# Five slots for split weights, a ring of five for raw data, and five half pieces at the end of a stage

## The chip, the cores and the metric

One core of one Trainium2 chip runs the whole program. The metric is device time in microseconds (us) of one execution; lower is better. The kernel before takes 2476.28 us, the median of three runs (2475.11 to 2478.31).

## The reference

Two layers of a decoder block on 256 tokens of width 2048, all in float32. `c_act` is `silu(c)`; `w_in` has 4,956 columns, which are cut into the inputs of three token mixers.

```python
def hybrid_layer(x, ...):
    mod = c_act @ ada_w + ada_b                      # 2048 x 12288 weights, one row of input
    sh_a, sc_a, gt_a, sh_m, sc_m, gt_m = jnp.split(mod[:, None, :], 6, axis=-1)
    h = rms_norm(x, norm_mix) * (1.0 + sc_a) + sh_a
    (cq, ckv, kr, fq, fk, fv, ff, nq, nkc, ...) = jnp.split(h @ w_in, split_points, axis=-1)
    o = concatenate([rms_norm(o_mla), rms_norm(o_fox), rms_norm(o_nsa)])   # three attentions
    x = x + gt_a * (o @ w_out)                       # 2048 x 2048
    h = rms_norm(x, norm_mlp) * (1.0 + sc_m) + sh_m
    u = jnp.square(jax.nn.relu(h @ mlp_w1))          # 2048 x 8192
    return x + gt_m * (u @ mlp_w2)                   # 8192 x 2048
# after two layers: rms_norm(x, final_norm)
```

## The kernel before

All weights are read once. They come in **pieces**: 256 rows by up to 512 columns, up to 512 KB, numbered Q = 0 to 827 in one order (`PIECES`, from `ORDER` and `mlp_order`). A layer has 158 pieces ahead of its MLP (`FRONT`: projections, compression weights `cw1`, output projection `wo0` to `wo3`) and 256 in the MLP.

A piece goes through four engines. SyncE (SP) issues its load into a slot of the raw ring `w_raw` (`load_piece`, L622). ScalarE (ACT) rounds it to the short format, `w_hi` (`hi`, L732). VectorE (DVE) computes the rest, `w_lo = w_raw - w_hi` (`lo`, L1197). TensorE (PE) multiplies in `product`: for both halves m of the 256 tokens and both groups of 128 rows three matmuls, `hi*hi`, `lo*hi`, `hi*lo` (L1668 to L1670), 12 matmuls in a piece; `cw1` pieces take 4 (`compress`, L1688 and L1689).

**Slots.** `w_hi` and `w_lo` have `RING` = 4 slots: `hi` of piece Q waits until PE has finished piece Q-4. `w_raw` has `RAW` = 7 slots, shared by the pieces and by the **ada tiles**, the 512 KB tiles of `ada_w` that DVE multiplies and accumulates itself (`ada_tile`, L1137, first of a block L1134). The load of an entry waits until DVE has consumed the entry `RAW` places earlier in the ring (`slot_free`), by `lo_done` or `ada_used`. `LOADS` sorts the loads by that moment. The first 64 ada tiles have eight slots of their own, and the first 24 pieces are never sorted ahead of `lo` of the piece five earlier.

**Order around a piece.** ACT and DVE run, after `hi(Q)` or `lo(Q)`, the steps listed under `SIDE[Q]`: evacuations, splits of transposed activations, attention steps (`slot`, `exp`), residuals, ada tiles. PE runs the transposes of `PE_POST[Q]` after piece Q. A transpose placed at q has its step on ACT and DVE at q+3 in nearly all cases. Each engine keeps its order, so a step that waits holds back everything behind it.

**Borders.** At the end of a stage (`BORDERS`: pieces 158, 414, 572, 828) the next stage needs the normalised result of the whole previous one. So the last four pieces are done by halves: first tokens 0 to 127 of all four (`product(q, (0,))`), which signals `half_done`, then tokens 128 to 255 of each. While PE does the second halves, `border` has the first half finished: residual (L1300, L1306), squares (ACT, L739), mean (L1166, L1167), power on GpSimd (POOL, L705), scaled copy (`fill`, L1192). PE transposes it (`n1_a` or `n2_a`, L1555) after piece B-2, ACT scales and rounds it (L771, L775), DVE takes the rest (L1311), and then PE starts the next stage: first halves of B, B+1, B+2, transposes of the second half (`_b`), first half of B+3, and then the second halves. The first piece of a stage also waits for its accumulator (`acc_free`): at 158 and 572 it is the one that the residual of the previous stage's last chunk has to leave (L1300 of m = 1); at 414 it is another.

Of the kernel before, what the change touches and what calls it, by code (L numbers as in the profile page):

```python
# [56 lines left out]
SUPERS = 4  # L57
MLP_LEN = SUPERS * 64
LAYER = FRONT + MLP_LEN
RING, RAW = 4, 7  # L60
ALL = LAYERS * LAYER


# [50 lines left out]
def side(Q, step, prio):  # L114
    SIDE.setdefault(Q, []).append((prio, len(SIDE[Q]), step))


def t_step(l, at, name, side_at, bank=0, prio=2, pre=False):

    (PE_PRE if pre else PE_POST).setdefault(at, []).append(("T", l, name))  # L120
    T_BANK[l, name] = bank
    side(side_at, ("T", l, name), prio)
# [17 lines left out]
def border(B, l, chunk, ln, which):  # L140


    side(B - 1, ("resid", l, chunk, 3, 0), 0)
    side(B - 1, ("square", ln, which, 3, 0), 0)
    side(B - 1, ("norm", ln, which, 0), 0)
    if which == "n1" and ln == LAYERS:
        side(B - 1, ("result", 0), 0)
        side(B, ("resid", l, chunk, 3, 1), 0)
        side(B, ("square", ln, which, 3, 1), 0)
        side(B, ("norm", ln, which, 1), 0)  # L150
        side(B, ("result", 1), 0)
        return
    side(B - 1, ("fill", ln, which, 0, 0), 0)
    t_step(ln, B - 2, f"{which}_a", B + 1, 0)
    side(B + 1, ("resid", l, chunk, 3, 1), 3)
    side(B + 2, ("norm", ln, which, 1), 3)
    side(B + 2, ("fill", ln, which, 0, 1), 3)
    side(B + 3, ("square", ln, which, 3, 1), 0)
    t_step(ln, B, f"{which}_b", B + 3, 1, 2, pre=True)
    side(B + 3, ("fill", ln, which, 1), 4)  # L160


for l in range(LAYERS):
# [5 lines left out]
    if l == 0:  # L169
# [4 lines left out]
        for b in range(1, 4):  # L174
            q = 6 * b
# [12 lines left out]
    if l:  # L188
        border(F, l - 1, (SUPERS - 1, 7), l, "n1")
        for b in range(1, 4):  # L190
            t_step(l, F + 6 * b - 5, f"n1_{2 * b}", F + 6 * b - 2, 0)
            t_step(l, F + 6 * b - 4, f"n1_{2 * b + 1}", F + 6 * b - 1, 1)
# [59 lines left out]


    border(M, l, "wo3", l, "n2")
    for b in range(1, 4):
        t_step(l, M + 6 * b - 5, f"n2_{2 * b}", M + 6 * b - 2, 0)
# [33 lines left out]
    for s in range(SUPERS):  # L290
        for j in range(4):
            q = M + 64 * s + 8 * (4 + j) + 10
            if s < SUPERS - 1 or j < 3:
                side(q, ("resid", l, (s, 4 + j), j), 3)
                if s == SUPERS - 1:
                    side(q + (2 if j < 2 else 1), ("square", l + 1, "n1", j), 4)
                    if l == LAYERS - 1:
                        side(q + 3, ("gain", j), 4)
border(ALL, LAYERS - 1, (SUPERS - 1, 7), LAYERS, "n1")

for Q in SIDE:
# [3 lines left out]
BORDERS = [FRONT, LAYER, LAYER + FRONT, ALL]  # L305
# [110 lines left out]
def trunk(nc, x, c, positions, inv_freq, ada_w, ada_b, norm_mix, norm_mlp, w_in, fox_b_f, mla_q_norm, mla_w_uq,  # L416
          mla_kv_norm, mla_w_ukv, nsa_pos_k, nsa_pos_v, cmp_k_w1, cmp_k_w2, cmp_v_w1, cmp_v_w2,
          out_norm, w_out, mlp_w1, mlp_w2, final_norm, out):
    with ExitStack() as ctx:
# [1088 lines left out]
        def _(pe):  # L1508
# [167 lines left out]
            def compress(Q):  # L1676

                l, chunk, p = PIECES[Q]
                j = p // 16
                if p == 0:  # L1680
                    pe.wait_ge(acc_free[1], ACC_USE[l, chunk])
                if p % 16 == 0:
                    pe.wait_ge(split_done, split_value(l, ("kcT", "vcT")[j]))
                pe.wait_ge(lo_done, Q + 1)
                for k in range(2):
                    kt = (p % 16) * 2 + k
                    st = BLK[j][:, 64 * kt:64 * kt + P]
                    pe.matmul(acc[1][:, j, :], st, w_hi[:, Q % RING, k, :], start=kt == 0, stop=False)  # L1688
                    mm = pe.matmul(acc[1][:, j, :], st, w_lo[:, Q % RING, k, :], start=False, stop=kt == 31)  # L1689
                mm.then_inc(piece_used, 1)  # L1690
# [57 lines left out]
            def then(Q):  # L1748

                for kind, l, what in PE_POST.get(Q, []):  # L1750
                    if kind == "csc":
                        compressed_scores(l, what)
                    elif kind == "T" and what != "csc":
                        t_in(l, what)
                    elif kind == "slot":
                        slot(l, what)

            for Q in range(ALL):
                if Q + 4 in BORDERS:
                    for q in range(Q, Q + 4):  # L1760
                        product(q, (0,))
                if Q in BORDERS:
                    for q in range(Q, Q + 3):
                        product(q, (0,))
                    for kind, l, what in PE_PRE[Q]:
                        t_in(l, what)
                    product(Q + 3, (0,))
                elif Q == 0:
                    for kind, l, what in PE_PRE[Q]:
                        t_in(l, what)  # L1770
                if any(B - 4 <= Q < B + 4 for B in BORDERS):
                    product(Q, (1,))
                elif PIECES[Q][1] == "cw1":
                    compress(Q)
                else:
                    product(Q)
                then(Q)
# [25 lines left out]
```

## Time and profile before

| | |
|---|---|
| median of the runs | 2476.28 us |
| the profiled execution | 2472.75 us |
| its span, first to last instruction | 2470.5 us |
| PE, DVE, ACT busy | 96%, 72%, 49% |
| mean granted TensorE clock | 0.989 |
| moved by DMA | 633.91 MB, mean 257 GB/s |

The span is what the profile's views divide; the execution's own time is 2.25 us more. A busy PE is modelled: consecutive 512-column matmuls start 0.23 us apart while each is listed with 0.39 us. In the timeline a bracket at the end of a row tells the idle time of that engine before the instruction and what ended it.

### The profile page before, as it was taken

How to read it: one execution, taken by the hardware profiler on the slowest of the kernel's cores; microseconds unless marked ns; L12 is line 12 of the kernel's file. 1: busy time of each engine (PE TensorE's matmuls, PEld its weight loads, DVE VectorE, ACT ScalarE, POOL GpSimd, SP SyncE). 2: the span in 40 equal slices, each digit the busy share in tenths (PEclk: the TensorE clock that was granted, in tenths of full speed). 3: DMA queues.
4: the chain of work that ended last, by engine and by line, in shares of the span. 5: the costliest groups of instructions: out<-in, count | busy, mean ns of one | idle time of the engine just before them, and what ended most of it. 6: DMA issues, size and time to landing. Idle time of an engine off the chain costs nothing.

```text
span 2470.5 us, 29668 instructions
## 1 busy us (share of the span) xinstructions
PE 2373.6 (96%) x11277; PEld 1969.3 (80%) x11277; DVE 1775.3 (72%) x2116; ACT 1203.5 (49%) x1646; POOL 23.7 (1%) x50
## 2 busy tenths in 40 slices
PE   3799999989999999999999999999999999999998
PEld 3677888768888888888878887878788888888887
DVE  7988988778777777887767788677566455555555
ACT  3256555445534434434445666455553453453453
POOL 1000000000000000000000000000000000000000
PEclk9899999999999999999999999999999999999999
DMA  9979986789889889888867788466577666666663
GB/s 368 382 242 351 314 281 210 256 292 324 286 306 308 291 317 323 304 316 300 296 228 266 264 268 281 137 213 213 180 253 256 188 186 195 185 185 197 187 188 127
DMA packets 318612, 633.91 MB, mean 257 GB/s; under 512 B 20428, under 2 KB 41352, under 8 KB 317832
## 3 DMA queue, kind: packets, MB, share of 16 engines
q1 hardware_dynamic: 314432, 625.49, 75.9%
q10 hardware_dynamic: 4040, 6.54, 0.8%
q8 instruction: 90, 1.47, 0.2%
q14 instruction: 50, 0.41, 0.0%
HBM read 629.85 MB, written 2.10 MB: 256 GB/s over the span
## 4 chain that ended last, share of the span: by engine, by line
PE 84%; DVE 8%; DMA 4%; issue 2%; ACT 2%; POOL 0%; SPq 0%; ACTq 0%; POOLq 0%; DVEq 0%
PE acc L1668 18%; PE acc L1670 18%; PE acc L1669 18%; PE pair L1668 7%; PE pair L1670 7%; PE pair L1669 7%; DMA arena<-in_ada_w 3%; DVE ada_acc L1137 3%; DVE w_lo L1197 2%; PE bank_T L1533 1%; PE bank_T L1578 1%; PE pair L1716 1%; PE bank_O L1533 1%; PE acc L1688 1%; PE acc L1689 1%
## 5 line engine op out<-in xcount | busy, mean ns | idle before, releaser
L1197 DVE TENSOR_TENSOR w_lo<-w_raw,w_hi 128x1024 fp32r<-128x1024 f32 (+3 forms) x828 | 981.5, 1192 | 376.7 <-ACT w_hi L732 376.0
L732 ACT ACTIVATE w_hi<-w_raw 128x1024 fp32r<-128x1024 f32 (+3 forms) x828 | 850.1, 1033 | 729.6 <-PE acc L1670 440.3
L1668 PE MATMUL acc<-w_hi,hT_hi 128*128 128x512 f32 (+3 forms) x1536 | 608.1, 396 | 24.8 <-DVE hT_lo L1311 12.7
L1670 PE MATMUL acc<-w_lo,hT_hi 128*128 128x512 f32 (+3 forms) x1536 | 589.4, 384 | 0.0
L1669 PE MATMUL acc<-w_hi,hT_lo 128*128 128x512 f32 (+3 forms) x1536 | 588.2, 383 | 0.0
L1137 DVE SCALAR_TENSOR_TENSOR ada_acc<-w_raw,silu_c,ada_acc 128x1024 f32<-128x1024 f32 x300 | 383.7, 1279 | 0.7 <-DVE small L1276 0.4
L1668 PEld LDWEIGHTS acc<-w_hi,hT_hi 128*128 128x128 f32 x1536 | 291.3, 190 | 85.3 <-DVE hT_lo L1311 15.6
L1670 PEld LDWEIGHTS acc<-w_lo,hT_hi 128*128 128x128 f32 x1536 | 290.8, 189 | 56.0
L1669 PEld LDWEIGHTS acc<-w_hi,hT_lo 128*128 128x128 f32 x1536 | 291.7, 190 | 51.6 <-issue 1.7
L1668 PE MATMUL acc<-w_hi,uT_hi 128*128 128x512 f32 (+1 forms) x720 | 283.0, 393 | 0.0
L1670 PE MATMUL acc<-w_lo,uT_hi 128*128 128x512 f32 (+1 forms) x720 | 279.6, 388 | 0.0
L1669 PE MATMUL acc<-w_hi,uT_lo 128*128 128x512 f32 (+1 forms) x720 | 279.4, 388 | 0.0
L1668 PE MATMUL pair<-w_hi,hT_hi 128*128 128x512 f32 (+1 forms) x448 | 178.6, 399 | 15.8 <-DVE w_lo L1197 15.8
L1670 PE MATMUL pair<-w_lo,hT_hi 128*128 128x512 f32 (+1 forms) x448 | 173.9, 388 | 0.0
L1669 PE MATMUL pair<-w_hi,hT_lo 128*128 128x512 f32 (+1 forms) x448 | 173.6, 388 | 0.0
L1669 PEld LDWEIGHTS acc<-w_hi,uT_lo 128*128 128x128 f32 x720 | 135.3, 188 | 27.8 <-issue 1.0
L1668 PEld LDWEIGHTS acc<-w_hi,uT_hi 128*128 128x128 f32 x720 | 135.2, 188 | 27.8 <-issue 1.0
L1670 PEld LDWEIGHTS acc<-w_lo,uT_hi 128*128 128x128 f32 x720 | 135.2, 188 | 27.8
L1668 PE MATMUL pair<-w_hi,uT_hi 128*128 128x512 f32 (+1 forms) x352 | 136.6, 388 | 1.5 <-DVE w_lo L1197 1.5
L1670 PE MATMUL pair<-w_lo,uT_hi 128*128 128x512 f32 (+1 forms) x352 | 136.2, 387 | 0.0
L1669 PE MATMUL pair<-w_hi,uT_lo 128*128 128x512 f32 (+1 forms) x352 | 136.1, 387 | 0.0
L1668 PEld LDWEIGHTS pair<-w_hi,hT_hi 128*128 128x128 f32 x448 | 86.0, 192 | 34.6 <-DVE w_lo L1197 19.0
(259 smaller groups left out, 2030.2 us busy)
## 6 DMA issues: line engine op xcount, KB each, us to landing
w_raw<-in_mlp_w SPq DMA_DIRECT2D x512, 512.0 KB, 4.8
w_raw<-in_ada_w SPq DMA_DIRECT2D x320, 512.0 KB, 5.7
w_raw<-in_w_in SPq DMA_DIRECT2D x112, 512.0 KB, 5.0
arena<-in_ada_w SPq DMA_DIRECT2D x64, 512.0 KB, 11.3
w_raw<-in_w_out SPq DMA_DIRECT2D x64, 512.0 KB, 5.6
w_raw<-in_nsa_cmp_k_w SPq DMA_DIRECT2D x32, 512.0 KB, 5.3
w_raw<-in_nsa_cmp_v_w SPq DMA_DIRECT2D x32, 512.0 KB, 5.2
w_raw<-in_w_in SPq DMA_DIRECT2D x16, 388.0 KB, 4.4
```

What stands on the lines that cost most here:

```text
L732: a.activation(w_hi[:, Q % RING, :, 0:n], w_raw[:, i % RAW, :, 0:n], ACT.Copy).then_inc(hi_done, 1)
L1137: ins = v.scalar_tensor_tensor(ada_acc[:], raw, silu_c[:, kt:kt + 1], ada_acc[:], ALU.mult, ALU.add)
L1197: v.tensor_tensor(w_lo[:, Q % RING, :, 0:n], w_raw[:, RING_NO["lo", Q] % RAW, :, 0:n], w_hi[:, Q % RING, :, 0:n].bitcast(F32), ALU.subtrac ...
L1533: mm = pe.transpose(bank[:, k, P * m:P * m + P], halves[m], ident[:])
L1578: mm = pe.matmul(flat_[:, k:k + 1], ada_acc[:, P * k:P * k + P], ones[:, 0:1], start=True, stop=True)
L1668: pe.matmul(o, st_hi[:, kt + k, tok], wh, start=first and k == 0, stop=False)
L1669: pe.matmul(o, st_lo[:, kt + k, tok], wh, start=False, stop=False)
L1670: mm = pe.matmul(o, st_hi[:, kt + k, tok], wl, start=False, stop=last and k == 1)
L1688: pe.matmul(acc[1][:, j, :], st, w_hi[:, Q % RING, k, :], start=kt == 0, stop=False)
L1689: mm = pe.matmul(acc[1][:, j, :], st, w_lo[:, Q % RING, k, :], start=False, stop=kt == 31)
L1716: mm = pe.matmul(o, NQ[:, h, qt], k_[:, h // 4, 0:keys], start=True, stop=True)
```

## The change

`RING` goes from 4 to 5 and `RAW` from 7 to 5: the memory for ten split tiles and five raw ones is that of eight and seven. At a border five pieces instead of four are done by halves, and the transpose of the first half moves from after piece B-2 to after piece B-3.

```diff
-RING, RAW = 4, 7
+RING, RAW = 5, 5
@@ border
-    t_step(ln, B - 2, f"{which}_a", B + 1, 0)
+    t_step(ln, B - 3, f"{which}_a", B + 1, 0)
@@ TensorE
             for Q in range(ALL):
-                if Q + 4 in BORDERS:
-                    for q in range(Q, Q + 4):
+                if Q + 5 in BORDERS:
+                    for q in range(Q, Q + 5):
                         product(q, (0,))
                 if Q in BORDERS:
                     for q in range(Q, Q + 3):
                         product(q, (0,))
...
-                if any(B - 4 <= Q < B + 4 for B in BORDERS):
+                if any(B - 5 <= Q < B + 4 for B in BORDERS):
                     product(Q, (1,))
```

## Rows read from the trace of the kernel before

**Rows 1.** The page: busy share by engine, and GB/s moved in 40 slices

```profile
PE 2373.6 (96%) x11277; PEld 1969.3 (80%) x11277; DVE 1775.3 (72%) x2116; ACT 1203.5 (49%) x1646; POOL 23.7 (1%) x50
...
GB/s 368 382 242 351 314 281 210 256 292 324 286 306 308 291 317 323 304 316 300 296 228 266 264 268 281 137 213 213 180 253 256 188 186 195 185 185 197 187 188 127
```

**Rows 2.** Waits of PE, whole run: total us, times, longest

```profile
PE pair L1668 <- DVE w_lo L1197: 17.3, 11, 3.5
...
PE acc L1668 <- DVE hT_lo L1311: 12.7, 7, 2.0
...
PE acc L1668 <- DVE w_lo L1197: 4.9, 6, 1.6
PE acc L1668 <- DVE ybuf L1300: 4.5, 2, 2.3
```

**Rows 3.** Timeline at the border of piece 414: start, us, engine, line

```profile
1278.64 0.39 PE L1668 MATMUL acc<-w_hi,uT_hi 128*128 128x512 f32 x1
...
1280.00 0.39 PE L1668 MATMUL acc<-w_hi,uT_hi 128*128 128x512 f32 x1
...
1281.65 0.69 DVE L1300 TENSOR_TENSOR ybuf<-acc,arena 128x512 f32<-128x512 f32 x1 [3.16 <-PE acc L1670]
...
1284.86 0.49 DVE L1192 TENSOR_SCALAR ybuf<-X,small 128x512 f32<-128x512 f32 x1 [0.65 <-POOL small L705]
...
1285.49 0.63 PE L1555 MATMUL bank_T<-ident,ybuf 128*128 128x128 f32 x4
...
1287.11 0.40 PE L1670 MATMUL acc<-w_lo,uT_hi 128*128 128x512 f32 x1
...
1289.21 0.47 PE L1668 MATMUL acc<-w_hi,hT_hi 128*128 128x512 f32 x1 [1.71 <-issue]
```

**Rows 4.** Timeline at the border of piece 572

```profile
1739.85 0.40 PE L1670 MATMUL acc<-w_lo,hT_hi 128*128 128x512 f32 x1
...
1741.77 0.68 DVE L1300 TENSOR_TENSOR ybuf<-acc,arena 128x512 f32<-128x512 f32 x1
...
1742.50 0.50 PE L1668 MATMUL acc<-w_hi,hT_hi 128*128 128x512 f32 x1 [2.26 <-DVE ybuf L1300]
```

**Rows 5.** Timeline ahead of the border of piece 158

```profile
534.46 3.48 DVE L1197 TENSOR_TENSOR w_lo<-w_raw,w_hi 128x1024 fp32r<-128x1024 f32 x3
...
535.73 0.50 PE L1668 MATMUL acc<-w_hi,hT_hi 128*128 128x512 f32 x1 [0.24 <-DVE w_lo L1197]
```

**Rows 6.** Windows: busy us by engine, PEclk, DMA share, GB/s

```profile
226.00:256.00 30.00, 29.34 (x174) 24.01 (x173) 27.84 (x38) 18.61 (x33) 0.00 (x0) 1.00 0.99 356
...
478.00:540.00 62.00, 58.27 (x263) 46.15 (x262) 51.48 (x52) 27.61 (x42) 0.69 (x1) 1.00 0.93 319
...
1950.00:2450.00 500.00, 500.00 (x2253) 413.84 (x2252) 266.10 (x229) 233.64 (x252) 0.00 (x0) 1.00 0.60 184
...
1297.00:1301.00 4.00, 4.00 (x12) 3.01 (x11) 1.27 (x2) 0.84 (x1) 0.00 (x0) 0.57 0.01 4
```

**Rows 7.** w_raw in windows 226:256 and 1950:2450, then timeline from 224

```profile
DMA to landing us min/median/max: 3.7/5.5/7.1
...
DMA to landing us min/median/max: 3.5/4.3/6.9
...
224.99 1.87 DVE L1197 TENSOR_TENSOR w_lo<-w_raw,w_hi 128x1024 fp32r<-128x1024 f32 x2
225.10 0.37 SPq L622 DMA_DIRECT2D w_raw<-in_nsa_cmp_k_w  x1
230.19 1.62 ACT L732 ACTIVATE w_hi<-w_raw 128x1024 fp32r<-128x1024 f32 x2 [0.82 <-DMA w_raw<-in_nsa_cmp_k_w]
231.28 1.88 DVE L1197 TENSOR_TENSOR w_lo<-w_raw,w_hi 128x1024 fp32r<-128x1024 f32 x2 [0.25 <-ACT w_hi L732]
```

**Rows 8.** Timeline of the last border (piece 828)

```profile
2460.01 0.74 DVE L1184 SCALAR_TENSOR_TENSOR X<-X,small,arena 128x512 f32<-128x512 f32 x1
...
2461.85 0.69 DVE L1300 TENSOR_TENSOR ybuf<-acc,arena 128x512 f32<-128x512 f32 x1 [1.09 <-PE acc L1670]
```

## The prediction

> **What bounds the kernel now.** I read the page first: PE is busy 96% of the span, DVE 72%, ACT 49%, and the GB/s row falls from 382 near the start to 185 in the second MLP [rows 1]. So the time is PE's work plus PE's gaps, and the reader should look only for gaps. The list of PE's waits [rows 2] gives them: 17.3 + 4.9 = 22.2 us for `w_lo` (supply of weights), 12.7 us for the split of a transposed activation (L1311) and 4.5 us for a residual that leaves an accumulator (L1300). Then the timeline at each border shows which wait ends last, and the windows show where supply is short. In 1950 to 2450 us PE is busy all the time at 184 GB/s [rows 6]: neither ring matters there. From 226 to 256 us DVE is busy 27.8 of 30 us and 356 GB/s move at a DMA share of 0.99; from 478 to 540 us it is 51.5 of 62 us, 319 GB/s and 0.93, with PE idle 3.7 us [rows 6].
>
> **The fifth half piece.** A first half is 6 matmuls, 1280.00 - 1278.64 = 1.36 us [rows 3]; call it h. No matmul is added, they change places. At the border of 414 `half_done` lets DVE start at 1281.65, the scaled copy ends at 1284.86 + 0.49 = 1285.35, and the transposes start at 1285.49, when PE has just done three second halves (3h = 4.1 us) [rows 3]: PE does not wait for them. After them PE has one second half (its last matmul starts at 1287.11) and then idles 1.71 us until 1289.21, when the split is there [rows 3]. With the change PE still has three second halves ahead of the transposes (B-5, B-4, B-3) and two behind. `half_done` and the whole chain come h = 1.36 us earlier against PE's finished work, the last second half ends where it did, and the wait shrinks from 1.71 to 0.35 us. Gain 1.36 us.
>
> At 572 the wait has another end. PE's last second half starts its last matmul at 1739.85, and the first piece starts at 1742.50 behind L1300, 1741.77 + 0.68 = 1742.45 [rows 4]. That is the residual of the second half, on the accumulator that the new piece needs; it can't start before PE ends its half, near 1740.2, but it sits behind the split L1311 on DVE. With the split h earlier it starts at 1741.77 - 1.36 = 1740.41, still behind PE's end: the full 1.36 us again, and 0.9 us of the 2.26 stay. Earlier by less than that would have been lost; earlier by more could not be had.
>
> At 158 PE waits at the end of the stage for `w_lo` itself: three splits run back to back from 534.46 to 537.94, and a first half waits 0.24 us at 535.73 [rows 5]. Five first halves can't end before the split of piece 157 (537.94) and two halves more, about where four end now. Value 0; bounds 1.4 us gained and 1.0 lost.
>
> At the last border the store chain of the first half ends at 2460.01 + 0.74 = 2460.75 and the second starts at 2461.85, when PE is done [rows 8]. The first was covered already: 0.
>
> Given back? The second half's chain (residual, squares, copy, transposes `_b`) hangs behind the same split on DVE and moves with it, so its wait stays. What the freed 1.36 us uncovers next is 0.35 and 0.9 us at the same spots.
>
> Clock: after the waits at 414 the granted clock is 0.57 of full speed over 1297 to 1301, mostly the level of 1.2 GHz instead of 2.4 [rows 6]: 12 matmuls in 4 us where 0.23 us each would be 2.8. With 1.36 us less idle ahead of it this fall may stay away. Bounds 0 and 1.7 us (half of a slow stretch of 3.4 us, 0.43/0.5 of the 4 us); value 0.3.
>
> **The fifth split slot.** `hi(Q)` may run when Q-5 is done. That frees ACT and DVE one piece earlier only where nothing else holds them; but a transpose at q has its step at q+3, and both engines wait there until PE is past q, so `hi(q+4)` is held as before. Where no such step stands (the MLP), PE doesn't wait today. The 22.2 us of `w_lo` waits lie where DVE is the busiest after PE (ada tiles at the start, 83% in 478 to 540 us [rows 6]); four or five slots don't change what DVE has to do. Value 0; at best it cures the 3.7 us of 478 to 540 [rows 6].
>
> **Five raw slots.** An entry's load now starts when the entry five earlier is consumed. With weights alone five entries last five pieces of 12 x 0.23 = 2.7 us, 13.7 us, against a landing of 4.3 us [rows 7]: nothing. With an ada tile beside each piece it is tight. In 226 to 256 us 356 GB/s x 30 us are 20 entries of 524,288 bytes, so five last 7.4 us. Worked example [rows 7]: the piece whose split starts at 231.28 is loaded by the issue at 225.10, seven entries back. Its fifth predecessor is the second split of the pair at 224.99, which ends at 226.86. Issued then (0.4 us of SP) and landed after 3.5 us (the shortest here: 3.5 and 3.7), it is there at 230.8, rounded (1.06 us) at 231.8: 0.5 us late for DVE. With the median landing of this stretch, 5.5 us, it is 2.5 us late. Landings grow with what is in flight (4.3 us at 184 GB/s, 5.5 at 356), and five slots put less in flight, so I take a value near the short one. A late entry costs DVE once in a round of five, and DVE has nothing to spare there, but PE still has its lead of 1 to 3 us. Four rounds at about 0.4 us are 1.6 us, of which PE feels most: 1.5 us. For the stretch 478 to 540, where nearly every third round is late, 0.3, and for the layer-1 front, with few ada tiles, 0.5. Sum 2.3 us. Bounds: 0, if every landing falls to 3.5 us and the lead takes the rest; and, with 2 us late in four rounds here, half of that in as many rounds around, and 1 us in the seven rounds or so of 478 to 540, 8 + 4 + 4 less the lead and the fifth split slot, 2 x 2.7: about 11 us.
>
> A word on the limit. The row shows 356 GB/s here and 382 in the second slice [rows 1, 6], 7% above. The Trainium skill (DMA: Bandwidth & Descriptors, Specifications) puts the HBM limit of one core at about 358 GB/s, and by that these 30 us are at the wall, each hole in the queue is lost for good, and the second rival below would be the likelier. The slice at 382 goes against it.
>
> **The sum.** Own time of the profiled execution 2472.75 (span 2470.5, 2.25 around it): - 1.36 - 1.36 - 0.3 + 2.3 = - 0.7, so 2472.0. The median of the runs, 2476.28, is 3.53 above that execution; the same change of it gives 2475.6 us. A difference of 0.2%, 5 us, is about what a measurement here can tell from none.
>
> **Rivals.**
> 1. The gain stays on the table (0.15). DVE still holds the split or the residual back, because `w_lo` of the next pieces, which the fifth slot lets run, now stands ahead of it; or the wait moves to the transposes of the second half. For it: L1300 ends the wait at 572 after a queue of DVE work [rows 4]. Against: ACT and DVE are idle ahead of each step of the chain (3.16 us at 1281.65, 0.65 at 1284.86) [rows 3]. Then only supply counts: 2476.28 + 2.3 = 2478.6.
> 2. Starved raw ring (0.22), the slower side. Place: 185 to 330 us and 478 to 540 us. It decides from the point where a landing takes over 4 us in a round of five lasting 7.4: then each round makes DVE late, and DVE, at 93% busy [rows 6], hands it on to PE. Price 9 us of the bound of 11. For it: 0.99 and 356 GB/s; against: fewer in flight land faster. 2476.28 - 2.7 + 9 = 2482.6.
> 3. Everything pays (0.13): h at three borders (4.1), the clock fall gone (1.7), no late entry. 2476.28 - 5.8 = 2470.5.
>
> **How the numbers follow.** My forecast, 2475.6, has the rest, 0.50, with a range of its own from 2472.5 to 2479. The range of 8 in 10 reaches into rivals 2 and 3: 2470.8 to 2484. Faster by over 5 us (under 2471.3) is most of rival 3 and a sliver of the forecast, 0.12; slower (over 2481.2) most of rival 2, 0.19; the rest, 0.69, is within.
>
> **What would show it.** Right: at 414 and 572 waits of about 0.35 and 0.9 us in place of 1.71 and 2.26, the waits for the split after the `_b` transposes (part of the 12.7 us) unchanged, first halves at 158 held by `w_lo`; landings in 226 to 256 us near 4 us instead of 5.5 and more ACT waits for DMA there; `w_lo` waits of PE in all some 2 us up. Wrong: `w_lo` waits up by 6 us or more (rival 2); L1300 or L1311 waits not shorter (rival 1); `w_lo` waits shorter than 22 us, which would mean that the fifth split slot does more than I grant it.

## The result, and the profile after

The kernel after takes 2508.84 us (median, 2504.76 to 2511.91), the one before 2476.48 beside it: ratio 1.0131, interval 1.0114 to 1.0148. It is 32 us slower, where I forecast 2475.6 and a range up to 2484. The profiled execution takes 2506.34 us with a span of 2504.1, 33.6 over the span before; TensorE's mean granted clock is 0.986 against 0.989.

The page after, answering [rows 1]: busy time by engine, and GB/s in 40 slices.

```profile
PE 2389.8 (95%) x11277; PEld 1974.5 (79%) x11277; DVE 1774.2 (71%) x2116; ACT 1192.8 (48%) x1646; POOL 23.7 (1%) x50
...
GB/s 367 360 241 318 291 294 202 241 288 266 300 286 332 299 287 332 291 296 319 294 259 244 250 287 274 135 220 201 180 249 272 187 183 200 182 190 195 177 195 140
```

The instruction counts are those of before: no work was added. Yet PE is listed as busy for 16.2 us more (2389.8 against 2373.6). Part of this is TensorE's clock: the missing share of the clock, 0.014 of 2504.1 us against 0.011 of 2470.5 us, is about 8 us more (an estimate). Two of the new falls, near 241 and 520 us, follow waits of PE of 1.83 and 2.78 us; no run here separates what such falls cost from what the waits cost. The peaks of supply are gone (382 to 360 in the second slice, 351 to 318 in the fourth). First I looked at the two borders, because that is where the diff says time should change. The PE rows of the timeline that answer to the last row of [rows 3] and of [rows 4], and DVE's L1300 ahead of the second:

```profile
1317.22 0.47 PE L1668 MATMUL acc<-w_hi,hT_hi 128*128 128x512 f32 x1 [0.35 <-issue]
...
1324.58 0.50 PE L1668 MATMUL acc<-w_hi,hT_hi 128*128 128x512 f32 x1 [1.92 <-DVE hT_lo L1311]
...
1775.27 0.69 DVE L1300 TENSOR_TENSOR ybuf<-acc,arena 128x512 f32<-128x512 f32 x1
...
1776.01 0.50 PE L1668 MATMUL acc<-w_hi,hT_hi 128*128 128x512 f32 x1 [0.90 <-DVE ybuf L1300]
```

The borders do what was forecast: 1.71 us became 0.35 and 2.26 became 0.90, and the wait behind the second half's transposes stays at 1.92. The loss lies elsewhere. PE's waits after, answering [rows 2] (total us, times, longest):

```profile
PE pair L1668 <- DVE w_lo L1197: 16.4, 12, 3.2
...
PE acc L1668 <- DVE hT_lo L1311: 12.8, 8, 1.9
...
PE acc L1668 <- DVE w_lo L1197: 12.5, 13, 1.7
PE acc L1688 <- DVE w_lo L1197: 8.4, 7, 1.9
```

`w_lo` waits of the pieces at L1668 went from 22.2 to 28.9 us, 6.7 us up, which is the sign that the prediction had named for its rival 2; the `cw1` pieces (L1688) wait 8.4 us, where it was 1.9. But a list of PE's waits names only who came last. One engine upstream it is far plainer. ScalarE's waits for a load, after:

```profile
ACT w_hi L732 <- DMA w_raw<-in_mlp_w: 360.1, 209, 5.9
...
ACT w_hi L732 <- DMA w_raw<-in_w_in: 81.0, 52, 5.7
...
ACT w_hi L732 <- DMA w_raw<-in_w_out: 50.1, 24, 7.8
...
ACT w_hi L732 <- DMA w_raw<-in_nsa_cmp_k_w: 35.8, 22, 5.3
```

and the same view of the kernel before:

```profile
ACT w_hi L732 <- DMA w_raw<-in_mlp_w: 39.2, 24, 3.1
...
ACT w_hi L732 <- DMA w_raw<-in_w_in: 29.4, 17, 5.5
...
ACT w_hi L732 <- DMA w_raw<-in_w_out: 17.0, 14, 4.5
```

These sums show where loads come late, not what that costs: 329.6 of the 360.1 us stand in the first MLP, which loses 6.3 us. To see where it costs time I matched the last matmul of each piece in the two traces. The table gives how many us later than in the kernel before it ends, for the kernel after and for kernels that come below.

| piece | 48 | 98 | 134 | 145 | 155 | 162 | 411 | 418 | 480 | 565 | 576 | 827 |
|---|---|---|---|---|---|---|---|---|---|---|---|---|
| after | 2.1 | 13.0 | 15.4 | 20.7 | 24.5 | 23.1 | 29.4 | 28.1 | 32.3 | 34.9 | 33.5 | 33.6 |
| r4w6 | -0.5 | 3.8 | 8.4 | 10.3 | 11.4 | 11.4 | 11.5 | 9.9 | 10.0 | 10.1 | 11.7 | 11.7 |
| after_halfada | -0.1 | 8.4 | 13.3 | 15.5 | 18.9 | 17.5 | 17.5 | 16.1 | 17.0 | 19.2 | 17.8 | 17.8 |
| tight_mid | -0.3 | 12.3 | 12.3 | 13.5 | 13.4 | 14.9 | 14.9 | 14.9 | 14.9 | 14.9 | 14.9 | 14.9 |
| lent2 | 1.2 | 2.2 | 2.2 | 3.0 | 3.0 | 4.6 | 4.6 | 1.7 | 1.7 | 1.7 | 0.3 | 0.3 |

Read from left to right: in the row of the kernel after the front of layer 0 loses 24.5 us, the first MLP (162 to 411) 6.3, the front of layer 1 (418 to 565) 6.8, the last MLP nothing: 37.6 us in all. The borders at 158, 414 and 572 give back 1.4, 1.3 and 1.4. Other steps of some 1.5 us at a border (r4w6 at 414 and 572, tight_mid at 158) are those of TensorE's clock (below). Everything lost is lost where ada tiles share the raw ring, and nothing where weights come alone.

**The loop, in the trace.** Timeline of the kernel after from 223.50 us, SP's issues, ACT's rounding, DVE's splits and ada tiles:

```profile
226.39 0.37 SPq L622 DMA_DIRECT2D w_raw<-in_nsa_cmp_k_w  x1
...
227.78 0.37 SPq L622 DMA_DIRECT2D w_raw<-in_w_in  x1
...
229.07 1.62 ACT L732 ACTIVATE w_hi<-w_raw 128x1024 fp32r<-128x1024 f32 x2 [4.16 <-DMA w_raw<-in_nsa_cmp_k_w]
...
230.16 1.88 DVE L1197 TENSOR_TENSOR w_lo<-w_raw,w_hi 128x1024 fp32r<-128x1024 f32 x2 [2.42 <-ACT w_hi L732]
...
231.42 0.34 SPq L641 DMA_DIRECT2D w_raw<-in_ada_w  x1
...
231.44 0.50 PE L1688 MATMUL acc<-w_hi,uT_hi 128*128 128x512 f32 x1 [1.95 <-DVE w_lo L1197]
...
232.42 1.62 ACT L732 ACTIVATE w_hi<-w_raw 128x1024 fp32r<-128x1024 f32 x2 [1.24 <-DMA w_raw<-in_nsa_cmp_k_w]
...
233.51 1.88 DVE L1197 TENSOR_TENSOR w_lo<-w_raw,w_hi 128x1024 fp32r<-128x1024 f32 x2 [0.28 <-ACT w_hi L732]
...
234.76 0.34 SPq L641 DMA_DIRECT2D w_raw<-in_ada_w  x1
...
237.00 1.62 ACT L732 ACTIVATE w_hi<-w_raw 128x1024 fp32r<-128x1024 f32 x2 [2.48 <-DMA w_raw<-in_nsa_cmp_k_w]
```

Follow one slot. It is given to the load issued at 226.39. The data is there at 232.42, when ACT, which stood still for it, starts; DVE starts at 233.51 and has consumed it at 233.51 + 1.22 = 234.73; at 234.76 SP issues the next load into it. One pass took 8.37 us, with ACT idle for 1.24 us and DVE for 0.28 us just before they took this slot. Lateness doesn't end with the entry: the late split is what issues the next load. In the kernel before, the window 226 to 256 us consumed 17 + 7 = 24 entries:

```profile
L1197 DVE TENSOR_TENSOR w_lo<-w_raw,w_hi x17: 731/1217/1226, 225.0 to 255.3; 128x1024 fp32r<-128x1024 f32 x9, 128x560 fp32r<-128x560 f32 x6, 128x776 fp32r<-128x776 f32 x2
...
L1137 DVE SCALAR_TENSOR_TENSOR ada_acc<-w_raw,silu_c,ada_acc x7: 1275/1279/1286, 226.8 to 252.9; 128x1024 f32<-128x1024 f32 x7
```

One each 1.25 us, so five must come round in 6.25 us and seven in 8.75. In the kernel after the same view of the same window counts 13 + 7 + 1 = 21:

```profile
L1197 DVE TENSOR_TENSOR w_lo<-w_raw,w_hi x13: 733/1218/1226, 230.2 to 255.9; 128x1024 fp32r<-128x1024 f32 x7, 128x560 fp32r<-128x560 f32 x6
...
L1137 DVE SCALAR_TENSOR_TENSOR ada_acc<-w_raw,silu_c,ada_acc x7: 1276/1279/1284, 226.5 to 254.5; 128x1024 f32<-128x1024 f32 x7
L1134 DVE TENSOR_SCALAR ada_acc<-w_raw,silu_c x1: 750/750/750, 225.6 to 225.6; 128x1024 f32<-128x1024 f32 x1
...
DMA to landing us min/median/max: 3.4/4.8/6.0
```

5 x 30 / 21 = 7.1 us for a pass, and the parts give 4.8 (median landing) + 1.05 (rounding) + 1.22 (split) = 7.07. The views count a landing from the start of its issue, so the 0.37 us of the issue are inside it; two of the expectations below add them once more. The window after, answering the first row of [rows 6], has DVE less busy, not more, and DMA less busy too:

```profile
226.00:256.00 30.00, 26.05 (x139) 21.32 (x138) 22.25 (x27) 15.11 (x25) 0.00 (x0) 0.89 0.90 306
```

The granted clock is 0.89 here, where it was 1.00. No engine is the bound here; the number of slots is.

### The profile page after: what moved, and what is told of

Same layout as the page of the kernel before. It is cut to its first block, busy times and chain, and to the rows that moved or that the text cites. A ratio compares the mean times of both kernels' runs of the same rounds, so it can differ in the third digit from the quotient of the medians.

```text
span 2504.1 us, 29667 instructions
## 1 busy us (share of the span) xinstructions
PE 2389.8 (95%) x11277; PEld 1974.5 (79%) x11277; DVE 1774.2 (71%) x2116; ACT 1192.8 (48%) x1646; POOL 23.7 (1%) x50
## 4 chain that ended last, share of the span: by engine, by line
PE 70%; DMA 11%; DVE 10%; ACT 5%; issue 4%; SPq 0%; POOL 0%; ACTq 0%; DVEq 0%; POOLq 0%
PE acc L1668 16%; PE acc L1670 15%; PE acc L1669 15%; PE pair L1668 5%; PE pair L1670 5%; PE pair L1669 5%; DMA w_raw<-in_mlp_w 4%; DVE ada_acc L1137 4%; DVE w_lo L1197 3%; ACT w_hi L732 2%; DMA w_raw<-in_w_in 2%; DMA arena<-in_ada_w 2%; DMA w_raw<-in_nsa_cmp_k_w 1%; PE bank_T L1578 1%; PE bank_T L1533 1%
## 5 line engine op out<-in xcount | busy, mean ns | idle before, releaser
L732 ACT ACTIVATE w_hi<-w_raw 128x1024 fp32r<-128x1024 f32 (+3 forms) x828 | 842.7, 1032 | 755.6 <-DMA w_raw<-in_mlp_w 360.1
L1668 PE MATMUL acc<-w_hi,hT_hi 128*128 128x512 f32 (+3 forms) x1536 | 611.0, 398 | 25.8 <-DVE hT_lo L1311 12.8
L1668 PEld LDWEIGHTS acc<-w_hi,hT_hi 128*128 128x128 f32 x1536 | 293.0, 191 | 89.3 <-DVE hT_lo L1311 15.8
L1668 PE MATMUL acc<-w_hi,uT_hi 128*128 128x512 f32 (+1 forms) x720 | 283.8, 394 | 2.8 <-DVE w_lo L1197 2.7
L1668 PE MATMUL pair<-w_hi,hT_hi 128*128 128x512 f32 (+1 forms) x448 | 178.6, 399 | 14.4 <-DVE w_lo L1197 14.4
L1668 PEld LDWEIGHTS acc<-w_hi,uT_hi 128*128 128x128 f32 x720 | 135.2, 188 | 32.8 <-DVE w_lo L1197 5.1
L1668 PE MATMUL pair<-w_hi,uT_hi 128*128 128x512 f32 (+1 forms) x352 | 136.9, 389 | 2.0 <-DVE w_lo L1197 2.0
L1407 DVE TENSOR_TENSOR uT_lo<-ybuf,uT_hi 128x512 fp32r<-128x512 f32 x64 | 44.3, 693 | 96.2 <-ACT uT_hi L856 96.2
```

What stands on the lines that cost most here:

```text
L732: a.activation(w_hi[:, Q % RING, :, 0:n], w_raw[:, i % RAW, :, 0:n], ACT.Copy).then_inc(hi_done, 1)
L1407: v.tensor_tensor(uT_lo[:, 2 * t:2 * t + 2, :], y_half(l, (s, t // 2), t % 2), uT_hi[:, 2 * t:2 * t + 2, :].bitcast(F32), ALU.subtract).th ...
L1668: pe.matmul(o, st_hi[:, kt + k, tok], wh, start=first and k == 0, stop=False)
```

## The experiments

Theory L is this loop: a stretch loses time where one pass of a slot (landing, issue included, then rounding and split) lasts longer than the slots' entries last at PE's pace. All ratios are to the kernel before, run beside them.

| kernel | us | ratio | interval |
|---|---|---|---|
| r4w5: 4 split pairs, 5 raw, old border | 2511.95 | 1.0144 | 1.0129 to 1.0159 |
| r5w5_b4: 5 and 5, old border | 2509.29 | 1.0134 | 1.0117 to 1.0151 |
| r4w6: 4 and 6, old border | 2483.16 | 1.0025 | 1.0014 to 1.0036 |
| after_bias162 | 2506.01 | 1.0120 | 1.0105 to 1.0135 |
| before_bias162 | 2473.53 | 0.9996 | 0.9987 to 1.0005 |
| before_halfada | 2472.79 | 0.9987 | 0.9977 to 0.9997 |
| after_halfada | 2491.62 | 1.0067 | 1.0052 to 1.0082 |
| after_quarterada | 2484.47 | 1.0036 | 1.0025 to 1.0048 |
| before_sparse | 2470.32 | 0.9986 | 0.9975 to 0.9996 |
| after_sparse | 2475.10 | 0.9991 | 0.9982 to 1.0000 |
| tight_mlp0 | 2480.46 | 1.0027 | 1.0015 to 1.0040 |
| tight_mid | 2487.20 | 1.0046 | 1.0032 to 1.0060 |
| lent2 | 2471.93 | 0.9977 | 0.9968 to 0.9986 |
| lent3 | 2475.30 | 0.9998 | 0.9989 to 1.0007 |

### One part at a time: r4w5, r5w5_b4, r4w6

```diff
-RING, RAW = 4, 7
+RING, RAW = 4, 5        # r4w5; 5, 5 in r5w5_b4, with four half pieces; 4, 6 in r4w6
```

r4w5: 

> The kernel before with five raw slots alone (RING 4, RAW 5, four half pieces, transpose after B-2). Theory A (the loss is the raw ring, the gain is the border): the raw ring costs 33.6 + 2.6 = about 36 us, since the changed kernel has earned h at two or three borders. So 2509 + 3 = 2511 to 2513 us, and the w_lo waits as in the changed kernel. Theory B (the fifth split slot does harm, for instance because rounding runs ahead and waits for a landing with other ScalarE work behind it): 2480 to 2495 us.

r5w5_b4: 

> The changed kernel with the border of before (RING 5, RAW 5, four half pieces, transpose after B-2). Theory A: slower than the changed kernel by 2 x 1.36 to 3 x 1.36 us, 2511 to 2513 us, equal to the kernel with RING 4, RAW 5 within 1 us: the fifth split slot itself does nothing. Theory B: clearly slower than RING 4, RAW 5. Theory C (the slot helps the lead): 5 us or more faster than RING 4, RAW 5.

r4w6: 

> RING 4, RAW 6, border of before. If each raw slot is worth the same, half of the 36 us: 2494 us. If there is a threshold between the round's length and landing plus rounding plus split, the sixth slot gives most of it back: 2480 to 2487 us, since a round of six entries is a fifth longer (8.9 us instead of 7.4 in the busiest stretch).

Five raw slots alone make the whole loss (r4w5, 35.0 us). The two kernels differ by 2.7 us in the medians, with intervals that overlap, and by 1.9 in the last matmul of the two traces (39.3 and 37.4 late). Of these, 1.5 is a fall of the clock behind piece 414 that r4w5 has and r5w5_b4 has not. So no gain of the fifth split slot is shown, and the nothing that I gave it may stand. The border's gain can't be told from noise in the medians (2509.29 and 2508.84); the waits above show it. The sixth slot gives back 29 of 35 us, and not half: this looks like a threshold, not a slope.

### Where the loss is made: tight_mlp0, tight_mid

```diff
-                if i >= RAW:
-                    before, k = IN_RING[i - RAW]
+                back = 5 if RING_NO["lo", 40] <= i < RING_NO["lo", 104] else RAW   # tight_mid
+                if i >= back:                       # tight_mlp0: from 158 to 414
+                    before, k = IN_RING[i - back]
```

tight_mlp0: 

> The kernel before (RING 4, seven raw slots in memory), where only the loads of the first MLP, pieces 158 to 413 and the ada tiles among them, wait for the entry five back instead of seven. Theory A: the loss is local and adds up by stretch; the changed kernel lost 6.3 us there, so 2481 to 2485 us. With four split slots the lead is one piece less, so up to 5 us more than that if the fifth split slot had covered part of it.

tight_mid: 

> The kernel before, but the loads of the ring entries from piece 40 to piece 104 of layer 0 wait for the entry five back in place of seven; all else as before. Theory L: the loss is made in the stretch itself, round by round, and kept to the end: the kernel after lost 10.9 us from piece 48 to 98, so + 8 to + 11, 2484 to 2488 us. Rival C (the kernel after lost there because it came in late from the stretch ahead, and needs the whole ring of five to build it up): under 5 us, 2477 to 2481.

Both keep all memory and the order of the loads of before, and make only the loads of one stretch wait for the entry five back. The first MLP costs 4.8 us (5.5 by the last matmuls from piece 162 to 411, where the kernel after lost 6.3), pieces 40 to 104 cost 11.2 by the medians, and in the table tight_mid loses 12.6 from 48 to 98 and 2.6 behind it, 1.5 of them by the clock at 158. The loss is local, it adds up, and nothing carried in is needed.

### The landing: before_halfada, after_halfada, after_quarterada

```diff
-                    sp.dma_start(w_raw[:, at, :, :], src).then_inc(raw_landed[at], 16)
+                    cols = 256 if RING_NO["ada", n] >= 30 else 512    # 128 in after_quarterada
+                    sp.dma_start(w_raw[:, at, :, 0:cols], src[:, :, 0:cols]).then_inc(raw_landed[at], 16)
```

before_halfada: 

> The kernel before, but every ada tile from the 31st entry of the raw ring on is loaded by half (256 KB instead of 512 KB; VectorE's work on it is unchanged, the other half is what the slot held). With seven slots supply binds only in 478 to 540 us and around 230 us: 2470 to 2476 us.

after_halfada: 

> The changed kernel with the same half loads of ada tiles. Theory A (five slots are short because a load takes 4.5 to 5.5 us to land with others in flight; fewer bytes land sooner): nearly all of the 33 us goes, and with the border gain it is level with or 1 to 4 us faster than the same edit on the kernel before, 2468 to 2478 us. Rival D (five slots are short by the fixed part of a landing and by the rounding and the split, whatever the bytes): 2490 us or more.

after_quarterada: 

> The kernel after with the ada tiles from the 31st ring entry on loaded by a quarter of their columns (it leaves out the other three quarters; VectorE's work and the number of ring entries are as in the kernel after). By half, 16 us of 34 stay in the trace. Theory L (the round of five is issue + landing + rounding and split, and the landing has a part that does not shrink with the bytes, 3.3 us for a load with none beside it): a landing near 3.7 us makes a round of 6.4 to 6.8 us, under the 7.4 of the busy stretches but not under their tightest rounds: 5 to 12 us stay, 2476 to 2484 us. Theory D (bytes in flight alone): the loss falls on in proportion, to about the border gain: 2471 to 2475. Theory O (the order of ACT and VectorE, not the landing, is what stays after the half): no change, 2489 to 2493.

I had expected the half tiles to cure the loss (2468 to 2478 us). They did not: 2491.62 us is in the range of the rival of that run, by which slots are short by the fixed part of a landing, the rounding and the split. The first MLP was cured wholly (17.5 at pieces 162 and 411), the front only in part. With quarter tiles the kernel is 8.0 us over the kernel before, and with the borders' 4.1 us added back some 12 are still lost. The 2484.47 us lie 0.5 above the range that I gave for theory L and 4.5 below that of theory O; the quarter tiles have no base of their own with seven slots. In the window 226 to 256 the landing shrinks slowly. The kernel with half tiles:

```profile
DMA to landing us min/median/max: 2.7/4.3/5.3
```

with quarter tiles:

```profile
DMA to landing us min/median/max: 2.4/3.8/5.1
```

The shortest landings of an ada tile there are 3.4, 2.7 and 2.4 us for whole, half and quarter tiles: 256 KB less saves 0.7 us, 384 KB less 1.0. By that, about 2 us (3.4 less twice 0.7, an estimate) don't depend on the bytes. The Trainium skill (DMA: Bandwidth & Descriptors, Anatomy of one DMA) fits one transfer as about 2.0 us + bytes / 436,000, for GpSimd's path; an estimate by that is 3.2, 2.6 and 2.3 us. These traces, of SP's path, agree within 0.2 us.

### Fewer entries, the same bytes: before_sparse, after_sparse

```diff
-IN_RING = [e for e in DVE_ORDER if e[0] == "lo" or e[1] >= FIRST_TILES]
+IN_RING = [e for e in DVE_ORDER if e[0] == "lo" or (e[1] >= FIRST_TILES and e[1] % 2 == 0)]
...
+                elif n % 2:
+                    raw = ada_acc[:]
```

before_sparse: 

> The kernel before with every second ada tile that goes through the raw ring (the odd ones) left out of the ring and not loaded; VectorE still runs its multiply-add for it, on its own accumulator, so its work is the same. It leaves out these tiles of ada_w. It is only the base for the next run. All theories: PE is not short of weights here, so 2471 to 2475 us, as with the tiles loaded by half (2472.8).

after_sparse: 

> The kernel after with the same tiles left out. It moves as many bytes as the kernel after with the ada tiles loaded by half (2491.6 us, 19 over its own base), but has fewer entries in the ring. Theory L (a loop: five slots pass one round in issue 0.4 + landing 4.3 to 4.8 + rounding and split 2.3 us, some 7.3 us, and whatever five entries last less than that is lost in every round): five entries, of which now one in four and not two in five is an ada tile, last over 9 us, so nearly nothing is lost: 0 to 6 us over its base less the 2.7 us of the borders, 2470 to 2478 us. Theory D (the bytes in flight, or DMA being late by itself): the bytes are those of the half tiles, so it loses what that kernel lost, 2488 to 2492 us.

2475.10 and not the 2491.62 of the half tiles with as many bytes; over their own bases with seven slots the two lose 4.8 and 18.8 us. That settles bytes against entries, for theory L. The cure is not whole: by the last matmuls, pieces 0 to 155 lose 7.0 us over the base (15.7 with the half tiles), and part of the rest is paid back at the borders. The landing did not even get shorter:

```profile
DMA to landing us min/median/max: 3.8/4.8/5.8
```

The pass is the 7.1 us of the kernel after, but five entries now last 5 x 30 / 19 = 7.9 us (15 splits and 4 ada tiles in its base). All kernels in one table, with a pass as median landing + 2.27, what the slots last at the base's 1.25 us an entry (1.58 for the sparse one), and the loss over the kernel before (over its own base the kernel with half tiles lost 9.5):

| kernel | slots | landing | a pass | slots last | lost, pieces 48 to 98 |
|---|---|---|---|---|---|
| before | 7 | 5.5 | 7.8 | 8.75 | 0 |
| r4w6 | 6 | 5.1 | 7.4 | 7.5 | 4.3 |
| after_sparse | 5 | 4.8 | 7.1 | 7.9 | 3.9 (over its base) |
| after_quarterada | 5 | 3.8 | 6.1 | 6.25 | 4.0 |
| after_halfada | 5 | 4.3 | 6.6 | 6.25 | 8.5 |
| after | 5 | 4.8 | 7.1 | 6.25 | 10.9 |
| tight_mid | 5 | 4.7 | 7.0 | 6.25 | 12.6 |

The order is roughly that of pass less "slots last": the three kernels whose pass is longer than that lose most. But three kernels whose median pass fits still lose about 4 us, which a median over one window can't explain. I take it that their longest landings there (6.4, 5.8 and 5.1 us for r4w6, after_sparse and after_quarterada) and bunched entries still make some rounds late; no run isolates that.

### The bias load: after_bias162, before_bias162

```diff
-    side(F + 143, ("bias", l), 4)
+    side(F + (143 if l else 162), ("bias", l), 4)
```

after_bias162: 

> The changed kernel with the 1 MB load of the MLP gate's bias of layer 0 moved from piece 143 to piece 162, where few loads are in flight. In the changed kernel TensorE lost 5.4 us at piece 144 while two weight loads took 8.3 and 8.6 us to land. Theory A1 (that load, beside five slots, made them late): faster than the changed kernel by 3 to 6 us, landings there 5 to 6 us. Theory A2 (only the slots): within 1 us of it.

before_bias162: 

> The kernel before with the 1 MB bias load moved from piece 143 to 162. With seven slots landings there take 6.7 to 8 us and TensorE waits 3.7 us for w_lo at pieces 149 to 155; those waits hang on VectorE, not on landings, so 2474.5 to 2476.5 us, no difference that can be told. If landings matter there, 2 to 3 us faster.

In the kernel after the load issued at 507.54 us lands 8.3 us after the end of its issue, while a 1 MB load of biases on ACT's own queue (issued at 506.28) is in flight. ACT, in order, stands at the rounding of piece 145, and the scaled copies of a transposed activation (L754) stand behind it:

```profile
516.22 1.06 ACT L732 ACTIVATE w_hi<-w_raw 128x1024 fp32r<-128x1024 f32 x1 [5.51 <-DMA w_raw<-in_w_out]
517.18 0.82 ACT L754 ACTIVATE arena<-bank_T,gcols 128x256 f32<-128x256 f32 x2
```

Moving the load away saves 2.8 us by the medians, between what the two theories gave and with intervals that overlap. In the trace the lag from piece 134 to 145 falls from 5.3 to 1.8 us, but from 98 to 134 it grows from 2.4 to 5.7, where 6.8 us at the lower level of the clock are new. From 98 to 155 the two kernels lose 11.5 and 11.3 us. So it is shown that a late landing holds ACT here, not that the move saves time. With seven slots the same move is within the noise.

### The border with its fifth pair lent: lent2, lent3

If the border is right and only the ring wrong, five pairs are needed for one piece per border and not for 828. These kernels have four pairs and seven raw slots, and round piece B-1 into two raw slots that the ring gives up for 15 entries.

```diff
+LENT = {B: (RING_NO["lo", B - 1] - 6, RING_NO["lo", B - 1] + 9) for B in FIVE}
...
+        if i0 <= i < i1:
+            allowed = range(5)
...
+    if Q + 1 in FIVE:
+        PAIR.append(4)          # w_hi, w_lo of piece B-1: raw slots 5 and 6
```

lent2: 

> Four pairs of split slots and seven raw slots as before, and yet five half pieces at the borders of pieces 414 and 572: the fifth piece is rounded into raw slot 6 and its rest goes into raw slot 7, which the ring gives up for 15 entries around the border. At 158 and at the end the old border. If the border's mechanism is right (waits of 1.71 and 2.26 us become 0.35 and 0.9) and the loss of the kernel after is the raw ring's alone: 2476.5 - 2.7 = 2473.8, 2472.5 to 2475. Rival: 15 entries with five slots ahead of 572, where ada tiles still run, cost as much as the border gives: 2476 to 2478.

lent3: 

> The lent fifth pair of split slots at three borders: 158 as well as 414 and 572, so raw slots 6 and 7 are also given up for 15 entries around piece 157, where four of them are ada tiles and the 1 MB bias load stands just ahead. If the border gain at 158 (wait 2.26 to 0.89 us in the kernel after) is there with seven raw slots too: 1.4 us under lent2, 2470.5 us. As I predicted for 158 (nothing, because PE waits for the split of piece 157): equal to lent2, 2471.9. If five slots for these 15 entries start the loss: 1 to 3 us over lent2, 2473 to 2475.

lent2 is faster than both kernels: 0.9977, 4.0 us under the kernel before. The timeline shows the borders of 414 and 572 as in the kernel after:

```profile
1279.05 1.04 ACT L780 ACTIVATE lent<-w_raw 128x1024 fp32r<-128x1024 f32 x1
...
1292.49 0.47 PE L1716 MATMUL acc<-w_hi,hT_hi 128*128 128x512 f32 x1 [0.35 <-issue]
...
1742.85 0.50 PE L1716 MATMUL acc<-w_hi,hT_hi 128*128 128x512 f32 x1 [0.91 <-DVE ybuf L1348]
```

That is below the range I gave for it (2472.5 to 2475), and only 2.7 of the 4.0 us are traced to these waits. Its profiled execution is not one in which they appear in the total (span 2470.8 against 2470.5): it came to piece 411 4.6 us late, 1.6 of them by a fall of the clock at 158, gained 2.9 at the border of 414 and 1.4 at that of 572. lent3 also shortens the wait at 158, and is slower than lent2: 0.9998 of the kernel before. PE's waits there, after one of ACT's waits for a load:

```profile
534.09 1.06 ACT L780 ACTIVATE w_hi<-w_raw 128x1024 fp32r<-128x1024 f32 x1 [3.26 <-DMA w_raw<-in_w_out]
...
530.89 0.50 PE L1716 MATMUL acc<-w_hi,hT_hi 128*128 128x512 f32 x1 [1.30 <-DVE w_lo L1245]
...
533.23 0.50 PE L1716 MATMUL acc<-w_hi,hT_hi 128*128 128x512 f32 x1 [0.68 <-DVE w_lo L1245]
...
536.46 0.50 PE L1716 MATMUL acc<-w_hi,hT_hi 128*128 128x512 f32 x1 [1.57 <-DVE w_lo L1245]
...
539.16 0.50 PE L1716 MATMUL acc<-w_hi,hT_hi 128*128 128x512 f32 x1 [1.05 <-DVE w_lo L1245]
...
550.43 0.50 PE L1716 MATMUL acc<-w_hi,hT_hi 128*128 128x512 f32 x1 [0.90 <-DVE ybuf L1348]
```

The border wait is 0.90 instead of 2.26, but 4.6 us of `w_lo` waits stand ahead of it, where the kernel before has the 0.24 of [rows 5] and this:

```profile
531.07 0.50 PE L1668 MATMUL acc<-w_hi,hT_hi 128*128 128x512 f32 x1 [1.30 <-DVE w_lo L1197]
```

In the trace it loses 3.5 us between pieces 145 and 155 and gains 1.4 at the border. Fifteen entries with five slots are enough to start the loop where ada tiles run.

## Why the prediction was wrong

**The failed step** is the term of the five raw slots: "I take a value near the short one", and then "Four rounds at about 0.4 us are 1.6 us". It was sized 2.3 us with a bound of 11, and measured 37.6 by the last matmuls, or 35.0 by the medians of r4w5. The place and the rough mechanism, rival 2's, were named, with a chance of 0.22; its price of 9 us was a quarter of the real one. Four things in the sizing were off:

1. **The landing.** I took 3.5 us. It is 4.8 in that window, where 306 GB/s for 4.8 us are 2.8 loads in flight. My worked example also added 0.4 us for the issue, which the views' landing holds already; that erred the other way. From the issues and landings of the kernel before (from 150 us on) one can read what I only guessed, the landing of a 512 KB load, counted here from the end of its issue (0.37 us less than in the views), by how many others are then in flight:

| in flight | 0 | 1 | 2 | 3 | 4 | 5 |
|---|---|---|---|---|---|---|
| median landing, us | 3.3 | 4.0 | 4.7 | 5.4 | 6.4 | 6.9 |

2. **The round.** I divided bytes by 524,288 and got 20 entries in 30 us, 7.4 us for five. The narrower pieces (128x560 in the row above) make it 24, and 6.25 us. With rounding and split the pass must fit into that, which leaves 4.0 us for the landing. That is the point of decision that I had named, but with a round of 7.4 us it would have been 5.1, and the 4.8 us would have fitted.
3. **A loop priced as an event.** My worked example came out 0.5 to 2.5 us late, and PE's steps at pieces 58, 62 and 63 (+2.2, +2.0, +2.9) are of that size. I let PE's lead of 1 to 3 us take most of it and counted four rounds. The bound has a slip as well: seven rounds at 1 us were added as 4, and with 7 it is about 14 us, still short. A lead is spent once; a pass that is too long recurs, and each late split issues the next load late. tight_mid shows 11 us from this stretch alone.
4. **The stretches counted.** I said that with weights alone five slots cost nothing, which holds in the last MLP (0.1 us). But the first MLP has ada tiles in the ring too, 177 entries in the 300 us from 600 in the kernel before, five in 8.5 us. On the average a pass fits into that; but from piece 194 to 210, where 2.5 of the 6.3 us are lost, five entries last 7.5 us and a pass lasts 8.1, with a median landing of 5.8. I counted 0. The layer-1 front lost 6.8, and I counted 0.5.

**What held.** The fifth half piece: 1.36 us at each of 414 and 572, waits 0.35 and 0.90, `_b` waits unchanged. **What I undervalued.** At 158 the wait fell from 2.26 to 0.89 us as well. My reason for nothing there (the splits of pieces 155 to 157 bound PE) was wrong for the wait behind L1300, though lent3 shows that the gain can't be had by taking raw slots. **The clock.** In the kernel after the fall behind 414 stayed:

```profile
1325.00:1329.00 4.00, 4.00 (x14) 3.07 (x13) 1.19 (x2) 0.00 (x0) 0.00 (x0) 0.62 0.42 112
```

and in lent2, with the same waits ahead, it was absent:

```profile
1300.40:1304.40 4.00, 4.00 (x26) 3.55 (x24) 1.13 (x2) 1.87 (x3) 0.00 (x0) 1.00 0.26 104
```

The rest of lent2's 2.9 us there, 1.5, is about my bound of 1.7. r4w6 has the old border, no fall and 1.6 us in the same place, so the shorter wait does not decide it. Of the nine profiled kernels with the old border at 414, five have the fall; of the seven with the new one, five. What decides it stays open.

The sentence on the HBM limit made rival 2 likelier by a wall at 358 GB/s. The loss came without that wall: the kernel after moves 306 GB/s in the window, and after_sparse lost far less with the landing as it was. What is left open: why single stretches (48 to 64, 126 to 134) lose unequally between kernels with the same slots, how much of the 37.6 us is the clock's, and 1.3 of the 4.0 us of lent2.

## What to carry to other kernels

Before a prefetch ring is cut, count its entries, not its bytes, in the busiest window, and compare the time that the remaining slots last with one whole pass of a slot: issue and landing with the loads then in flight, and every consumer up to the release. If the pass is longer, the stretch runs at the pass's pace for as long as it lasts, and no lead of the last engine pays for more than the first round. When a buffer is needed at a few moments only, lend it there, and not where the ring is tight.

## What the runs showed of the hardware

A 512 KB load with none beside it lands 3.3 us after the end of its issue (median, kernel before), and each further load in flight adds about 0.7 us (table above). Of the 3.4 us, issue included, of the shortest whole ada tile in the kernel after, about 2 us don't shrink with its size (an estimate from the half and quarter tiles). A load of 512 KB issued 1.3 us behind a 1 MB load from another queue took 8.3 us from the end of its issue.
